# Four passages of a network's residual stream: warm-up products, a first slab in token halves, and a norm's sum and root moved into feed-forward

## The reference

```python
for layer in range(2):
    u = rms_norm(x, gains[layer, 0]);  mix = mixer[layer](u)
    x = x + rms_norm(mix, gains[layer, 1])
    u = rms_norm(x, gains[layer, 2]);  ff = conv_ffn(u, ...)
    x = x + rms_norm(ff, gains[layer, 3])
# then second_block(x): rmsnorm, projections, attention

def conv_ffn(u, w_up, conv_w, conv_b, w_down):      # d_ff 2816, 3 taps along the tokens
    gate, val = split(causal_dwconv(u @ w_up, conv_w) + conv_b, 2)
    return (silu(gate) * val) @ w_down
```

## Time and profile before

| | us |
|---|---|
| median of 3 runs | 1761.88 (1760.64 to 1762.17) |
| profiled execution, its own time | 1760.09 |
| its span in the profile | 1758.3 |
| TensorE busy | 1694.6 (96%) |
| VectorE busy | 1082.2 (62%) |
| ScalarE busy | 852.2 (48%) |
| GpSimd busy | 433.6 (25%) |
| mean granted TensorE clock | 0.993 of full speed |

### The profile page before, as it was taken

The page is one execution under the profiler, slowest core; times in us unless marked ns, Lnnn a source line. Parts: engine busy times, 40 slices in busy tenths (PEclk is TensorE's granted clock), DMA queues, the critical chain, the costliest instruction groups (busy, mean ns, idle before and its releaser), DMA issues. The chain is left out here.

```text
span 1758.3 us, 23786 instructions
## 1 busy us (share of the span) xinstructions
PE 1694.6 (96%) x8312; PEld 1385.9 (79%) x8312; DVE 1082.2 (62%) x1690; ACT 852.2 (48%) x1456; POOL 433.6 (25%) x334
## 2 busy tenths in 40 slices
PE   7999999999999999899999999999999989999997
PEld 5787887878888888778888887888888876777775
DVE  5636454377666643588788858766663367887353
ACT  5657545454333332456555645433332255365573
POOL 0444454201111100125654630111110012232232
PEclk9999999999999999999999999999999999999999
DMA  5321111222222223311211212222223223121121
GB/s 207 114 72 73 37 37 67 73 78 97 96 98 97 90 98 98 115 48 61 72 61 61 73 48 80 96 99 96 95 85 106 96 96 112 48 84 61 48 73 48
DMA packets 40516, 144.78 MB, mean 82 GB/s; under 512 B 4578, under 2 KB 4834, under 8 KB 39924
## 3 DMA queue, kind: packets, MB, share of 16 engines
q1 hardware_dynamic: 40436, 143.72, 23.7%
HBM read 141.57 MB, written 2.13 MB: 82 GB/s over the span
## 5 line engine op out<-in xcount | busy, mean ns | idle before, releaser
L187 PE MATMUL bank<-u_high,w_high 128*128 128x512 f32 x1580 | 644.6, 408 | 11.5 <-DVE m_on L1940 3.2
L189 PE MATMUL bank<-u_high,w_low 128*128 128x512 f32 x1580 | 618.8, 392 | 0.0
L188 PE MATMUL bank<-u_low,w_high 128*128 128x512 f32 x1580 | 617.0, 390 | 0.0
L187 PEld LDWEIGHTS bank<-u_high,w_high 128*128 128x128 f32 x1580 | 298.4, 189 | 82.3 <-issue 24.1
L189 PEld LDWEIGHTS bank<-u_high,w_low 128*128 128x128 f32 x1580 | 297.1, 188 | 64.7
L188 PEld LDWEIGHTS bank<-u_low,w_high 128*128 128x128 f32 x1580 | 298.3, 189 | 59.0 <-issue 4.1
L151 ACT ACTIVATE w_high<-w_ring 128x1024 fp32r<-128x1024 f32 x233 | 244.1, 1053 | 200.4 <-PE bank L189 176.6
L160 DVE TENSOR_TENSOR w_low<-w_ring,w_high 128x1024 fp32r<-128x1024 f32 x176 | 220.5, 1257 | 169.4 <-ACT w_high L151 169.2
L160 POOL TENSOR_TENSOR w_low<-w_ring,w_high 128x1024 fp32r<-128x1024 f32 x57 | 136.6, 2407 | 449.6 <-ACT w_high L151 449.5
L881 ACT ACTIVATE conv_up<-bank,col_sb 128x512 f32<-128x512 f32 x88 | 68.6, 779 | 270.6 <-DVE bank L936 270.6
L996 POOL TENSOR_TENSOR hidden<-conv_up 128x512 f32 x44 | 58.1, 1322 | 492.3 <-DVE conv_up L947 373.8
(11 more groups left out here) (420 smaller groups left out, 2289.9 us busy)
## 6 DMA issues: line engine op xcount, KB each, us to landing
w_ring<-ffn_up SPq DMA_DIRECT2D x88, 512.0 KB, 3.5
w_ring<-ffn_down SPq DMA_DIRECT2D x44, 512.0 KB, 3.4
w_ring<-c_in SPq DMA_DIRECT2D x32, 512.0 KB, 3.5
w_ring<-g_in SPq DMA_DIRECT2D x16, 512.0 KB, 3.5
w_ring<-m_in SPq DMA_DIRECT2D x12, 512.0 KB, 7.2
w_ring<-fox_in SPq DMA_DIRECT2D x12, 512.0 KB, 4.8
w_ring<-dsa_in SPq DMA_DIRECT2D x12, 512.0 KB, 3.4
w_ring<-ab_out SPq DMA_DIRECT2D x8, 512.0 KB, 4.0
```

The source lines that it names most:

```text
L187: nc.tensor.matmul(out, a[0], b[0], start=start, stop=False)
L188: nc.tensor.matmul(out, a[0], b[1], start=False, stop=False)
L189: return nc.tensor.matmul(out, a[1], b[0], start=False, stop=stop)
```

## The change

- `Opening.warm`: eight products of 128x512 on weights that lie ready, into bank 3, which is free; they are issued between the mixer's sums with ones and the first slab. Their result is not used.
- `Opening.project`, in the four passages (`extra` is 1): slab 0's high products go in two token halves, each with its own wait, instead of waiting for both; slab 1 too has its high products ahead of its low ones.
- The last square before the mixer's sums goes in two token halves, and the sums with ones are ordered by half. In `ffn` the gathers stand between the copies of the banks.
- In `half_out` alone (`later`): the sum with ones and the root of the next norm leave the Opening. VectorE gathers one square, splits w0, gathers two more, splits w1. The four other gathers, the sum (now in bank 7, inside feed-forward's first tile, before its last two slabs), and the root are done in `ffn`; VectorE waits for the root before the first "taken". The splits of slots 2 and 3 move ahead of it. The squares lie in `k.y` instead of `mx`.

```diff
+WARM = 8
@@ Opening
+    def warm(self, pe):
+        k = self.k
+        k.wait_split(pe, self.tile + 1)
+        for _ in range(WARM):
+            k.nc.tensor.matmul(k.ps[3][:, :], k.ws[0][0][:, 0:P], k.ws[1][0][:, 0:T], start=True, stop=True)
+
+    def sum(self, pe):
+        k = self.k
+        pe.wait_ge(self.gathered, KD - 1)
+        k.nc.tensor.matmul(self.bank[:, :], k.c("ones"), k.rn[:, :], start=True, stop=True).then_inc(self.summed, 1)
@@ Opening.project
-                if m == 0:
-                    pe.wait_ge(self.u_high, 1 + self.extra)
-                    for j in js:
-                        k.wait_split(pe, self.tile + j)
-                        s = self.slots[j]
-                        for n in range(2):
-                            k.nc.tensor.matmul(k.ps[s][:, :], k.ws[s][n][:, 0:P], k.uh[:, 0, :], start=n == 0, stop=False)
-                    pe.wait_ge(self.u_low, 1)
+                if m <= self.extra:
+                    parts = 1 + self.extra if m == 0 else 1
+                    w = T // parts
+                    for i in range(parts):
+                        pe.wait_ge(self.u_high, 1 + i if m == 0 else m + 1 + self.extra)
+                        c = slice(w * i, w * i + w)
+                        for j in js:
+                            s = self.slots[j]
+                            if m == 0:
+                                k.wait_split(pe, self.tile + j)
+                            for n in range(2):
+                                k.nc.tensor.matmul(k.ps[s][:, c], k.ws[s][n][:, m * P:m * P + P], k.uh[:, m, c],
+                                                   start=m == 0 and i == 0 and n == 0, stop=False)
+                    pe.wait_ge(self.u_low, m + 1)
...
-            if j == 1:
+            if j == 1 and not self.later:
...
-                pe.wait_ge(self.gathered, KD - 1)
-                k.nc.tensor.matmul(k.ps[4][:, :], k.c("ones"), k.rn[:, :], start=True, stop=True).then_inc(self.summed, 1)
+                self.sum(pe)
@@ half_out and ffn, TensorE
-            pe.wait_ge(squared, KD)
-            for i, c in enumerate(parts):
+                pe.wait_ge(squared, KD + i)
                 nc.tensor.matmul(k.ps[i][:, c], k.c("ones"), square(KD - 1)[:, c], start=False, stop=True).then_inc(summed, 1)
+            op.warm(pe)
@@ half_out and ffn, ScalarE
-                nc.scalar.activation(square(m), (mx[:, m, :] if m < held else k.ps[m][:, :]), ACT.Square).then_inc(squared, 1)
+                for c in (parts if m == KD - 1 else [slice(0, T)]):
+                    nc.scalar.activation(square(m)[:, c], (mx[:, m, c] if m < held else k.ps[m][:, c]), ACT.Square).then_inc(squared, 1)
@@ half_out, ScalarE
-            op.root(act)
@@ half_out, VectorE
-            op.gather(dve, lambda m: mx[:, m, :])
-            for j in range(2):
-                op.split_low(dve, j)
+            op.gather(dve, lambda m: k.y[:, m, :], 1, 2)
+            op.split_low(dve, 0)
+            op.gather(dve, lambda m: k.y[:, m, :], 2, 4)
+            op.split_low(dve, 1)
@@ ffn, TensorE, group 1
+                    elif s == 0:
+                        k.project(bank(i, s)[:, :], s, None, 0, KD - 2)
+                        opened.sum(pe)
+                        k.project(bank(i, s)[:, :], s, None, KD - 2, KD).then_inc(k.proj_done, 1)
+                        continue
+                    elif s == 3:
+                        pe.wait_ge(opened.rooted, 1)
@@ ffn, ScalarE, ahead of group 0
+            for s in range(2):
+                high(1, s + 2)
+            opened.root(act)
@@ ffn, VectorE, ahead of group 0
+            opened.gather(dve, lambda m: k.y[:, m, :], 4)
+            for s in range(2):
+                k.split_low(dve, s + 2, 6 + s)
+            dve.wait_ge(opened.rooted, 1)
@@ ffn, VectorE, copies and gathers
+            for m in range(held):
+                dve.wait_ge(kt.mixed, m + 1)
+                nc.vector.tensor_copy(mx[:, m, :], k.ps[m][:, :]).then_inc(moved, 1)
+                if m > 1:
+                    gather(m - 1)
+            for m in range(held - 1, KD - 1):
+                gather(m)
```

More of the change, by code:

```diff
@@ L115, in __init__ @@
         self.ahead = self.split = 0
+        self.pending = None
         self.ps = [nc.alloc_psum_tensor(f"bank{i}", [P, T], F32) for i in range(8)]
@@ L233, with __init__ @@
 class Opening:
[L238 to L242, removed]
+    def __init__(self, k, tag, gain, slots, turns, tile, product, extra=0, later=False):
+        self.k, self.gain, self.slots, self.turns, self.tile, self.product, self.extra, self.later = k, gain, slots, turns, tile, product, extra, later
+        self.u_high, self.u_low = k.sem(f"u_high_{tag}"), k.sem(f"u_low_{tag}")
+        sem = k.nc.alloc_semaphore if later else k.sem
+        self.squared, self.gathered, self.summed, self.chained, self.rooted = self.kept = [
+            sem(f"{s}_{tag}") for s in ("x_squared", "x_gathered", "x_summed", "x_chained", "x_rooted")]
+        self.bank = k.ps[7] if later else k.ps[4]
     def high(self, act, m, lo=0, hi=T):
@@ L255, in square, with gather @@
         k.nc.scalar.activation(out, k.x[:, m, :], ACT.Square).then_inc(self.squared, 1)
-    def gather(self, dve, square):
+    def gather(self, dve, square, first=1, last=KD):
         k = self.k
-        for m in range(1, KD):
+        for m in range(first, last):
             dve.wait_ge(self.squared, m + 1)
@@ L267, in root @@
         act.wait_ge(self.summed, 1)
-        Chain(act, self.chained).link(k.nc.scalar.activation(k.rn[:, :], k.ps[4][:, :], ACT.Ln, bias=k.epsc[:, 0:1], scale=1.0 / D))
+        Chain(act, self.chained).link(k.nc.scalar.activation(k.rn[:, :], self.bank[:, :], ACT.Ln, bias=k.epsc[:, 0:1], scale=1.0 / D))
         k.nc.scalar.activation(k.rn[:, :], k.rn[:, :], ACT.Exp, scale=-0.5).then_inc(self.rooted, 1)
@@ L280, in project @@
             for m in ms:
-                if m == 0:
-                    pe.wait_ge(self.u_high, 1 + self.extra)
-                    for j in js:
-                        k.wait_split(pe, self.tile + j)
-                        s = self.slots[j]
-                        for n in range(2):
-                            k.nc.tensor.matmul(k.ps[s][:, :], k.ws[s][n][:, 0:P], k.uh[:, 0, :], start=n == 0, stop=False)
-                    pe.wait_ge(self.u_low, 1)
+                if m <= self.extra:
[12 more added lines that the diff above has]
+                    pe.wait_ge(self.u_low, m + 1)
                     for j in js:
                         s = self.slots[j]
-                        k.nc.tensor.matmul(k.ps[s][:, :], k.ws[s][0][:, 0:P], k.ul[:, 0, :], start=False, stop=False)
+                        k.nc.tensor.matmul(k.ps[s][:, :], k.ws[s][0][:, m * P:m * P + P], k.ul[:, m, :], start=False, stop=False)
                     continue
@@ L582, in half_out @@
     mx = k.sb(f"mixed_sb_{tag}", [P, KD, T])
-    op = Opening(k, tag, gain_next, (0, 1, 2, 3), (2, 2, 2, 2), KD, KD - 2, 1)
+    op = k.pending = Opening(k, tag, gain_next, (0, 1, 2, 3), (2, 2, 2, 2), KD, KD - 2, 1, True)
     moved, squared, gathered, summed, rooted, scaled, added, ln_done = (
@@ L645, in _ @@
                 op.high(act, 0, c.start, c.stop)
-            op.square(act, 0, mx[:, 0, :])
+            op.square(act, 0, k.y[:, 0, :])
             for m in range(1, KD):
@@ L649, in _ @@
                 op.high(act, m)
-                op.square(act, m, mx[:, m, :])
-            op.split_high(act, 0)
-            op.split_high(act, 1)
-            op.root(act)
+                op.square(act, m, k.y[:, m, :])
+            for j in range(2):
+                op.split_high(act, j)
         @block.vector
@@ L773, in ffn @@
     nc, sem = k.nc, k.sem
+    opened, k.pending = k.pending, None
     k.retire()
@@ L789, in ffn @@
     k.clear_retired()
+    k.sems += opened.kept
     held = KD // 2
@@ L866, in step @@
                 for s in range(4):
-                    if start and s < 2:
-                        high(1, s + 2)
-                    elif s < 2 and not after:
+                    if s < 2 and not start and not after:
                         high(i, s + 2)
@@ L936, in step @@
                     nc.vector.tensor_tensor(bank(i, s)[:, :], bank(i, s)[:, :], k.rn[:, :], ALU.mult).then_inc(taken, 1)
-                    if start and s < 2:
-                        k.split_low(dve, s + 2, 6 + s)
-                    elif s < 2 and not after:
+                    if s < 2 and not start and not after:
                         k.split_low(dve, s + 2, 4 * i + s + 2)
@@ L959, in _, with gather @@
             kt.low(dve)
[L960 to L963, removed]
+            def gather(m):
                 dve.wait_ge(squared, m + 1)
```

## The result

The changed kernel takes 1772.34 us in the median (1771.69 to 1772.70, 4 runs) against 1761.26 for the kernel before on the same chip: 11.1 us slower, ratio 1.0061, 95% interval 1.0047 to 1.0074. The forecast was 1773. The profiled execution has a span of 1770.4 us, 12.1 over the one before.

A forecast was written before the change was run, and what follows sets the result against it. TensorE, busy 96% of the span, was taken as the bound. 2 x 4.8 (A, C) + 2 x 0.1 (B, D) + 1.7 (clock) = +11.5 us gave 1771.6 profiled, 1773 median; range 1764 to 1778.5.

The forecast's parts named there:

- The stall: Feed-forward after A and C: TensorE waits for w_low and takes tile 8 3.1 us later than before.
- feed-forward 2.5 us sooner: Border after passage A: feed-forward starts at 396.0, 2.5 us sooner than before.
- first "taken": Start of feed-forward: VectorE's first tile scaling, waiting for the root, at 402.65, 4.2 us later than before.
- idle time: TensorE ahead of feed-forward's second group: done with tile 7 at 418.6, then idle for 4.7 us.
- R1: Rival, not slower: VectorE catches up and tile 8's split is ready in time; 1759 us, or 1756; chance 0.12.
- The clock behind it: TensorE behind the late second group after A and C: low clock after the idle time, +1.7 us each.
- R2: Rival: the late second group without the low clock, +6.4 us, 1768 us; chance 0.15.
- B and D: Passages at the ends of ffn "0" and "1": gain hidden behind VectorE's last gather, +0.1 us each, 2.5 us wait.
- The fall of the clock there: Low clock behind the new idle time, taken in one of B and D: +1.7 us.
- A and C: Passages of half_out "ab" and "c" with the feed-forward after each: +4.8 us each, bounds +2.2 and +6.5.
- Products of 256 columns: Slab 0's sixteen high products in the opening: 0.13 us each, 2.1 us together; bounds 0.113 and 0.2266 each.
- The warm-up: Eight products ahead of the opening fill TensorE's idle time, so the low clock goes: 1.7 us gained for TensorE.

The follow-up runs named there:

- Experiment 3: Changed kernel with the rounding and split of the weights of tiles 8 and 9 moved into group 0, behind "taken" of tiles 2 and 3; 1761.92 us.
- experiment 4: Changed kernel with 18 unused 128x512 products issued between tile 7 and the wait for tile 8; 1768.05 us.
- experiment 5: Changed kernel without the eight warm-up products; 1772.81 us.
- experiment 11: Kernel before the change with one edit: the sum with ones stands behind tile 2 in the four passages; 1760.03 us.
- experiment 1: Changed kernel with the sum and root put back into the opening of half_out; 1765.33 us.
- experiment 8: Kernel of experiment 1 without the warm-up products; 1765.68 us.
- experiment 6: Kernel of experiment 1 with the sum with ones behind tile 2 instead of tile 1 in the four passages; 1755.69 us.
- experiment 9: Kernel of experiment 6 without the warm-up products; 1755.88 us.
- experiment 10: Kernel of experiment 6 with the old first slab (one wait for all 512 tokens, slab 1 waiting for its low part), warm-up kept; 1755.78 us.
- experiment 7: Kernel of experiment 3 with the sum behind tile 2 in passages B and D; 1757.79 us.
- experiment 2: Changed kernel without warm-up products and with the old first slab; 1775.48 us.

## Why the prediction was right

**The stall.** This was the term of 3.1 us, and it measured 3.05 and 3.06, with the steps in between where they were put: feed-forward 2.5 us sooner, first "taken" 6.64 us behind the border (6.65 forecast), the split of 2.10 us behind the seventh "taken", idle time 4.48 (4.7). Experiment 3 shows the cause and not only the place: with the rounding and the split of two tiles moved and nothing else the stall is gone. One reading was off by a little: tile 8 of the kernel before started at 420.37 and not at 420.24, the end of the stretch in which the 96 products start, so the slack was 0.3 us and not 0.2, in A and in C. R1 was wrong in one thing, that a backlog which shrinks 2 us a tile is soon harmless. It need only last for eight tiles.

**The clock behind it.** 1.7 us a time was too low: 2.35 and 2.96 by the offsets of the trace, 4.9 together by experiment 4. The forecast took the length of the low stretches behind idle times of 3.2 and 3.6 us in one execution. That length is no constant: behind 4.5 us it was 4.7 and 6.1 us here and 3.4 and 5.4 in experiment 5, and behind 3.6 us 5.55 in experiment 11. R2, the stall without its clock, would have been experiment 4's 1768.05; it had been put at 1768.

**B and D.** +0.1 us each is what the trace shows (the same instructions 6.08 us late before the passage and 6.15 behind it), with a wait of 2.17 us against 2.5 forecast. The fall of the clock there, put at one of two, came in neither in the profiled execution, which offset the term above. That the total came out so close is luck in this part: A and C cost 11.4 us where 9.6 were forecast, B and D nearly nothing where 1.9 were. Whether the clock falls there differs from execution to execution: experiments 1, 3, 4 and 8 show the fall behind this very wait in one of four, one of two, none of two and three of three places. What the forecast read from one row, that 2.01 us of idle time leave the clock up, does not hold: in experiment 1 the same wait was followed by the low clock, and so it was in seven of the thirteen profiled executions of this document. That the clock was low from the first product on in A, but in B only 1.4 us behind it, was also read too coarsely: in B it was low from 745.09, 1.0 us behind the first product.

```profile
316.25 0.47 PE L189 MATMUL bank<-u_high,w_high 128*128 128x512 f32 x1 [2.00 <-DVE w_low L568]
```
```profile
316.80:321.00 4.20, 4.20 (x21) 3.86 (x20) 0.00 (x0) 1.80 (x4) 0.00 (x0) 0.59 0.38 125
```

**Products of 256 columns.** The trace has them 0.12 us apart (373.14, 373.26). 0.13 was taken; the rule of the Trainium skill, TensorE: Matmul & The Clock Gate, section "Back-to-back issue gap", gives 0.109 for an isolated one; the trace lies between the two. The split beside GpSimd's multiply took 2.10 us in its new place too (421.87, the multiply 0.25 us before it), as the rule of the Trainium skill, SBUF — State Buffer, section "Who interferes with whom", has it when GpSimd starts first:

```profile
421.62 1.27 POOL L1038 TENSOR_TENSOR hidden<-conv_up 128x512 f32 x1 [4.70 <-DVE conv_up L980]
```

**What was not foreseen** is where the gain lay. The forecast said that the gain of B and D is hidden behind the gather and stopped there. The same row tells that six products may be moved ahead of it: experiment 6 is that, and it brings 5.4 us. The warm-up was taken at its face value of 1.7 us for TensorE; where VectorE's gather ends the opening, experiments 8 and 9 find nothing of it beyond the noise. Of warm-up and halves either will do: experiments 9 and 10 leave out one each and lose 0.6 and 0.5 us over their own kernel before, no more than the noise; with neither (experiment 11) 4.7 us of the 5.4 are missing in the median. Experiment 11 also has the last square whole and the gathers behind the copies, as in the kernel before. No experiment takes out these two alone, so their share is not shown.

What also stays open: how much of the spread of experiment 11's runs, 5.6 us, the clock makes, since only one of them is shown by stretches, and whether the distance between experiments 6 and 7 beyond the 1.7 us of waits is real.

## What to carry to other kernels

When a result is moved over a border, count what is queued behind its first reader, up to the first instruction for which the bounding engine waits; a slack of 0.3 us there is the number that decides, not the busy share of 62%. A bounding engine made faster at the start of a stretch only arrives earlier at the wait that ends it; look there for independent work to put ahead of the wait before the start is tuned. The two idle times of 4.5 us were paid twice here, once in the split that came too late (6.2 us) and once in the clock behind it (4.9 us), and filler products recovered the second part alone.

## What the runs showed of the hardware

The low clock followed the idle times of TensorE of 3.0 to 4.5 us ahead of openings and second groups in every place but one: behind 3.13 us in experiment 2 the clock stayed at 1.00. Behind 2.0 to 2.5 us it came in some executions and not in others, with the same instructions: the 2.0 us at 316 left it at 1.00 in the kernel before and at 0.59 in experiment 1. Where it came, the low clock lasted for 3.4 to 6.1 us of work in the places named above. In the two kernels with the 2.2 us wait and the sum in all four openings (experiments 1 and 8), runs of one kernel differed by 6.1 and 3.1 us; without such a wait (experiment 6) by 1.6.
